# Stick-breaking heads: the first triangle product of a head pair issued after, instead of before, the second half of a step's fill

## The reference, cut to what matters

```python
z = jnp.einsum('bqhd,bkhd->bhqk', qi, k).astype(jnp.float32) * scale
strict = kpos[None, :] < qpos[:, None]
log_1mb = jnp.where(strict, jax.nn.log_sigmoid(-z), 0.0)
between = lax.cumsum(log_1mb, axis=3, reverse=True) - log_1mb
a = jnp.where(strict, jnp.exp(jax.nn.log_sigmoid(z) + between), 0.0)
return jnp.einsum('bhqk,bkhd->bqhd', a.astype(v.dtype), v)
```

## Time and profile before

| | us |
|---|---|
| median of 3 executions | 2298.75 (2298.23 to 2299.9) |
| the profiled execution, its own time | 2297.43 |
| its span | 2295.6 |
| PE busy | 2286.1 |
| DVE busy | 1607.3 |
| ACT busy | 1041.6 |

### The profile page before, as it was taken

How to read it: one execution, slowest core, us unless ns; L and a number is a source line. 1 busy time by engine, 2 the same in 40 slices (tenths; PEclk the granted TensorE clock), 3 DMA queues, 4 the chain that set the end, 5 groups by cost and what they waited for, 6 DMA issues and landing times.

```text
span 2295.6 us, 31946 instructions
## 1 busy us (share of the span) xinstructions
PE 2286.1 (100%) x12088; PEld 1900.6 (83%) x12088; DVE 1607.3 (70%) x2989; ACT 1041.6 (45%) x1962; POOL 0.2 (0%) x4
## 2 busy tenths in 40 slices
PE   9999999999999999999999999999999999999998
PEld 7888888998888888998877788888887778888887
DVE  7788768775578777775577668567567777668565
ACT  5456544443346544443567533223246764223222
POOL 0000000000000000000000000000000000000000
PEclk9999999999999999999999999999999999999999
DMA  5333333342343333334231242424313113422422
GB/s 177 109 107 106 96 78 116 110 141 98 128 121 106 103 95 110 107 95 156 74 89 56 67 138 74 138 65 129 129 33 103 47 47 102 148 92 82 133 65 97
DMA packets 81688, 233.19 MB, mean 102 GB/s; under 512 B 16064, under 2 KB 16960, under 8 KB 80768
## 3 DMA queue, kind: packets, MB, share of 16 engines
q1 hardware_dynamic: 81392, 230.89, 33.0%
q10 hardware_dynamic: 144, 0.26, 0.0%
HBM read 209.48 MB, written 4.20 MB: 93 GB/s over the span
## 4 chain that ended last, share of the span: by engine, by line
PE 99%; DVE 0%; DMA 0%; ACT 0%; SPq 0%; issue 0%; DVEq 0%
PE bank L656 24%; PE bank L658 23%; PE bank L657 23%; PE bank L1569 3%; PE bank L1568 3%; PE bank L1567 3%; PE bank L2631 2%; PE bank L2633 2%; PE bank L2632 2%; PE bank L1430 2%; PE bank L2448 1%; PE bank L2416 1%; PE bank L1414 1%; PE bank L2432 1%; PE bank L590 1%; PE bank L1403 1%
## 5 line engine op out<-in xcount | busy, mean ns | idle before, releaser
L656 PE MATMUL bank<-h_hi,w_hi 128*128 128x512 f32 x1696 | 672.7, 397 | 0.2
L658 PE MATMUL bank<-h_lo,w_hi 128*128 128x512 f32 x1696 | 661.4, 390 | 0.0
L657 PE MATMUL bank<-h_hi,w_lo 128*128 128x512 f32 x1696 | 661.1, 390 | 0.0
L1278 DVE TENSOR_TENSOR w_lo<-raw_w,w_hi 128x1024 fp32r<-128x1024 f32 x296 | 358.4, 1221 | 88.5 <-ACT w_hi L1266 85.9
L1266 ACT ACTIVATE w_hi<-raw_w 128x1024 fp32r<-128x1024 f32 x295 | 309.7, 1054 | 181.2 <-DMA raw_w<-w_dram 173.2
L656 PEld LDWEIGHTS bank<-h_hi,w_hi 128*128 128x128 f32 x1696 | 318.7, 188 | 70.2 <-issue 7.6
L658 PEld LDWEIGHTS bank<-h_lo,w_hi 128*128 128x128 f32 x1696 | 318.4, 188 | 68.0
L657 PEld LDWEIGHTS bank<-h_hi,w_lo 128*128 128x128 f32 x1696 | 318.9, 188 | 61.0
L2868 ACT ACTIVATE nrm<-bank 128x512 f32<-128x512 f32 x44 | 26.3, 599 | 285.6 <-PE bank L658 285.6
L3265 DVE TENSOR_TENSOR ytmp<-nrm,bank 128x512 f32<-128x512 f32 x26 | 17.9, 688 | 117.0 <-PE bank L658 116.9
L1733 ACT ACTIVATE prob<-prob,small 128x128 f32<-128x128 f32 (+3 forms) x128 | 70.8, 555 | 61.6 <-DVE small L882 61.6
(11 more groups left out here) (443 smaller groups left out, 4539.8 us busy)
## 6 DMA issues: line engine op xcount, KB each, us to landing
raw_w<-w_dram SPq DMA_DIRECT2D x276, 512.0 KB, 3.6
down_raw<-w_dram SPq DMA_DIRECT2D x36, 512.0 KB, 4.5
raw_w<-w_dram SPq DMA_DIRECT2D x36, 256.0 KB, 3.0
proj_raw<-w_dram SPq DMA_DIRECT2D x36, 256.0 KB, 3.0
extra_raw<-w_dram SPq DMA_DIRECT2D x10, 512.0 KB, 4.8
x<-x_dram SPq DMA_DIRECT2D x8, 512.0 KB, 6.4
k_lo<-k_lo SPq DMA_DIRECT2D x32, 128.0 KB, 2.3
ln_row<-row_dram SPq DMA_DIRECT2D x4, 1024.0 KB, 6.4
```

The costliest lines, as they stand in the source:

```text
L656: nc.tensor.matmul(dst, lh, rh, start=start, stop=False)
L657: nc.tensor.matmul(dst, ll, rh, start=False, stop=False)
L658: return nc.tensor.matmul(dst, lh, rl, start=False, stop=stop)
L1278: nc.vector.tensor_tensor(lo_of(u), raw_of(u), hi_of(u).bitcast(F32), ALU.subtract) \
```

## The change

The product of the step before is held back where that step is the first of a stick-breaking pair (j = 0, steps 16 and 20), and issued behind the second half of the fill and behind the late work of steps 17 and 21. It happens once for each pair, so twice a layer and four times in the program, each time with the products of two heads. No instruction is added or removed on any engine, and ACT, DVE and SP keep their orders.

```diff
@@ -2546,13 +2546,16 @@
-                if step and not beside:
+                behind = is_sb(step - 1) and (step - 1) % NB == 0
+                if step and not beside and not behind:
                     between(step - 1)
                 if step == TAIL + 3:
                     out_block(OUT_FILL[step], NB - 1, (1,))
                 fill(step, 1)
                 if step in LATE:
                     late_work(LATE[step])
+                if behind:
+                    between(step - 1)
                 for own in group[1:]:
                     fill(own, 0)
                     fill(own, 1)
```

## The result

The changed kernel takes 2302.02 us (median of 22 executions, 2301.22 to 2302.84) against 2298.5 us for the kernel before, measured beside it (22 executions): 3.5 us more, a ratio of 1.0015 with a 95% interval of 1.0009 to 1.0021. The forecast was 3.66 us more. The interval excludes a change of nothing, and its upper end lies just at the 0.2% (4.6 us) that the prediction named.

What follows compares the result with a forecast made beforehand. PE was taken to bound the kernel; 1.42 us (first pair) and 0.41 us (second), times 2 layers, gave 3.66 us on 2298.75, so 2302.4 us. Forecast's own range about 2301.0 to 2304.3; stated range 2299.5 to 2305.4.

Steps and rivals of the forecast that it cites:

- What bounds the kernel: Whole kernel: PE, busy 2286.1 of 2295.6 us, with no wait to remove; whatever makes PE wait is paid in full.
- The move itself: PE in steps 17 and 21: fill following fill saves 0.08 us a place, 0.3 us in four places if nothing waited.
- the second 0.08 us: Step into the scores on PE: kept as a cost; by the skill's rule it would go too, 0.16 a place.
- The first wait: Scores of steps 18 and 22 wait for ACT's exponentials: 0.45 us in the first pair, 0.41 in the second.
- The late low part: Head 1's product of step 18 waits for DVE, late through ACT's queue: 0.86 plus 0.11 us for the weight load.
- The second pair: Steps 20 to 22: ACT's lag does not get through, with 0.74 us of slack on DVE; only 0.41 us lost.
- D: Rival: the lag reaches head 1's product of step 22 too; 1.42 us in all four places, 5.7 us, 2304.4; chance 0.17.
- B: Rival: only the four waits for the exponentials are paid, ACT's lag dies before step 18's product; 1.7 us, 2300.5; chance 0.15.
- C: Rival: no wait at all, exponentials out in time; gain of 0.08 us a place, 0.3 us, 2298.4; chance 0.08.
- the line L2461 <- ACT: Sign in PE's waits, scores waiting for the exponentials: 4 times, 1.4 to 1.8 us in all.
- L2476: Sign in PE's waits, product waiting for DVE's low part: twice, 0.5 to 0.9 us each, or split over two heads.

Runs made afterwards that it cites:

- before_values: Kernel before, with the product of steps 16 and 20 moved earlier, right behind the next step's raw scores, ahead of values and first half fill: 0.5 us over before (1.0003).
- copy_first: Changed kernel, with ACT's output copy and squares put ahead of the exponentials in steps 17 and 21: 1.64 us over the kernel before (1.0007).
- second_pair: Kernel before, with only the second pair's product (step 20) of each layer moved behind the second half fill: 0.5 us over before (1.0002).
- first_pair: Kernel before, with only the first pair's product (step 16) of each layer moved behind the second half fill: 3.0 us over before (1.0013).

## Why the prediction was right

**What bounds the kernel**: right. PE had no wait to remove in these steps, and each microsecond of wait came out in the time in full.

**The move itself**: the products moved by nine slots, 2.06 us as forecast: head 1's from 1216.82 to 1219.70 with the scores of step 17 0.83 us later, so 2.05. The 0.08 us that it should save is hidden inside the wait, and no run showed it alone; the same holds for the second 0.08 us, of the scores' weight load. In before_values, without a wait, the sequence of full and half-array products cost more, not less.
By the Trainium skill's rule that weight loads are pulled ahead of running matmuls where row groups don't conflict or the load goes to the background buffer ("TensorE: Matmul & The Clock Gate", "Step-by-step: what each phase is for"), 0.16 us a place would have been saved. The trace agrees with the rule inside the fill (the load of L657 starts at 1217.05, its matmul at 1217.28), but the load of the half-array scores starts with them, and no run here shows any saving beside half-array products.

**The first wait**: forecast 0.45 and 0.41 us, measured 0.43 (copy_first, D1) and 0.39 to 0.40 (D2 of second_pair and of the change). The scores start where the sum put them: 1219.64 + 0.83 = 1220.47, measured 1220.46. The 0.05 us from DVE to PE, taken for ACT to PE, holds: 1220.13 + 0.28 = 1220.41 to 1220.46.

**The late low part**: forecast 0.86 + 0.11, so 1.42 with the first wait; measured 1.31 to 1.35. The term that was too large is the lag: 2.06 was taken to arrive whole at the Ln of head 1, but it arrived as 1226.11 - 1223.31 - 0.83 = 1.97. Most of the other 0.09 was slack at the tile copy. It was 1.99 us late where the square ahead of it was 2.04: in the kernel before it started at 1219.30, 0.03 us behind the end of the last fill matmul (1218.88 + 0.39 = 1219.27), so it had waited for that. The slack lies within the 0.2 us that the window of the earlier trace rows leaves outside busy time, and which I had put down to gaps between dependent instructions. DVE's window gave back its 0.17 as taken: L3147 comes at 1231.93 - 1229.31 - 0.83 = 1.79, 0.18 less than 1.97. The uncovered weight load behind a wait was 1232.83 - 1232.54 = 0.29 against 0.18 in the kernel before: 0.11, as taken.

**The second pair**: right in size (0.40 against 0.41), and by its reason: ACT's copy there ran into the old idle time. That ACT's lag does not get through was right; how near another path stood was not told. The prediction spoke of 0.74 us of slack on DVE, true for the Ln of head 1, but on the path over scores, mask and DVE, head 1's low part ended only 0.12 us ahead of its product. Nor did the prediction have what DVE carries from the first pair into the second: it stays hidden in the changed kernel, and first_pair shows it with 0.13 us.

**The rivals**: D (all places as the first) is out by second_pair; B (only the first wait) by D1, which is 1.35 and not 0.43 us longer; C (no wait) by the four waits for ACT. The stated range, 2299.5 to 2305.4 us, takes in B and D as well, so it is the distances and the experiments that bear the forecast's account out, not the median alone. **The signs named**: the line L2461 <- ACT came as forecast, 4 times and 1.5 us. For L2476 I had named 0.5 to 0.9 us twice (or split over the heads), and the profile shows 0.2 twice. The wait is there, but it is split: head 0's product was already held from 1231.20 (its old place, 1229.92, plus both shifts) to 1231.48, 0.05 us behind its own low part:

```profile
1230.87 0.56 DVE L3147 TENSOR_TENSOR sp_low<-rope_a,act_hi 128x384 fp32r<-128x384 f32 x1
```

No bracket stands there, since the idle time counts from the modelled end of the matmul before. What the profile would print was wrong, not the cost. And the span of the profiled execution is 0.9 us longer than the places explain; 0.83 of that lies ahead of step 17, where executions differ by up to 1.5 us without any change.

## What to carry to other kernels

When a product is moved behind its cover, look past the engine that waits for it directly: count how late the next engine's queue becomes, subtract its idle time, and find the first product on the bounding engine that hangs on that queue; the slack there decides, as a threshold. What lies below it can still be carried on by a third engine, as DVE did into the second pair. Cover taken from the step ahead is not free either, since it delays whatever starts that step's own chain. And measure such changes by distances between two starts in the trace: they held to 0.03 us where medians of 11 executions left 2 us.

## What the runs showed of the hardware

Two full-precision products of 128x128 cost 0.36 us between fills of 128x512 and 0.64 us between products on half the array's rows and half its columns (before_values: 1214.72 to 1215.36). I had expected that place to be the cheaper one. The granted clock was 0.999 to 1.0 in every run, through waits of 0.4 us, so the waits brought no slower clock; the waits for a low part cost themselves and 0.06 us (second pair) to 0.11 us (first pair) for the weight load behind them.
